# A two-layer Mamba-2 / gated-MLP encoder step on one core: one residual step, one row of mixer units and two sets of norm sums change places

## Chip, cores and metric

The kernel runs on one core of one Trainium2 chip. The metric is the device time of one execution in microseconds (us), the median over several runs.

## What is computed

One inference step over 576 frames: 512 of a new stream and 64 of a running one. Two layers, each a token mixer and a squared-ReLU feed-forward network (FFN), each followed by a residual and a LayerNorm. Cut to what matters here (float32 throughout, `x` is 576 x 1024):

```
# layer 0: Mamba-2 state-space mixer, 8 groups of 4 heads
proj = x @ w_in; z, xbc, dt = split(proj)
xbc  = silu(causal_conv4(xbc) + b)
y, h = ssd_scan(xs, softplus(dt + dt_bias), A, B, C, h0)     # chunked scan
g    = (y + d * xs) * silu(z)
g    = g * rsqrt(mean(g*g over the group) + eps) * norm_w
x    = layer_norm(alpha * x + g @ w_out)                      # norm 0
x    = layer_norm(alpha * x + square(relu(x @ w1)) @ w2)      # norm 1
# layer 1: chunked spatial-gating mixer
u, v = split(gelu(x @ w_in + b_in)); v = layer_norm(v)
s    = tril(w_s) @ v (per 128-row block and group) + b_s
x    = layer_norm(alpha * x + (u * s) @ w_out)                # norm 2
x    = layer_norm(alpha * x + square(relu(x @ w1)) @ w2)      # norm 3
```

## The kernel before

**Layout.** Features lie on the 128 partitions, the 576 frames (`T`) along the free axis, split into two halves of 288 (`HT`). A weight unit is 128 x 1024: eight 128 x 128 blocks. Each float32 operand is split into a high and a low part, and TensorE (PE) makes a product of three matmuls: high by high, weight-high by data-low, weight-low by data-high (`products`, L627 to L629). A unit is therefore 2 halves x 8 blocks x 3 = 48 matmuls of 288 columns.

**PSUM slots.** Unit `u` writes the slot `u % 2`: two banks, 0 and 1 or 2 and 3. Before it starts, PE waits until its weights are split (`w_ready`) and until the unit two before it has been read out of the slot (`slot_evac0` or `slot_evac1`). Banks 4 to 7 serve the state-space chunks, the spatial products and the sums of the norms. Weights come from HBM through SP's queue into a ring of four buffers; POOL splits them from the last state-space group on.

**Order.** Every engine has its own program, written out by hand, and works through it strictly in that order; semaphores tie them together. Three places matter.

*The last state-space group* (`group(GROUPS - 1, False)` in the programs of VectorE, DVE, and of PE). While the last chunks run, PE already computes the first units of `w_out` (`U_WOUT + 0` to `+ 5`, `nxt(j)` in PE's `group`). DVE reads each of them out with `residual_first` (L1617 adds the slot to alpha times the input's high part and frees the slot, L1620 adds the low part). After the last chunk (`after(g, 4)`, up to L1579) DVE runs `gate` (L1591, y * silu(z)), then the residual step of unit 3, then `sum_squares` (L1596), which waits for ScalarE's (ACT's) square of the gated rows. PE's unit 5 needs the slot of unit 3. PE's `mean_squares(g)` follows its unit 5 and needs `sum_squares`.

*The mixer of layer 1* (end of PE's program, `mix`, `norm_v`, `uv_low` on DVE, `u_gelu`, `uv_round` on ACT). `gate_unit(k)` gives the u columns of tile k, `spatial(k)` (L936 to L938, small float32 matmuls into banks 4 to 7) the mixed v columns. PE runs gate unit 2, the row sums of the spatial weights (L946), then for k = 0 to 15: the gate unit k+1 from k = 2 on, the first unit of the output product, `U_CMOUT`, at k = 15, and `spatial(k)`. For each k DVE runs `mix(k)` (L2027, L2030, L2032, L2038), then `norm_v(k + 2)` (L2012), which makes the operand of a later `spatial`, and, once ACT has rounded the product (L1350), `uv_low(k)` (L2044). Only behind the whole loop stands DVE's `block(U_CMOUT, "first")`, which reads out the units of the output product with the same `residual_first` (L1617, L1620):

```
    for k in range(16):
        mix(k)
        ...
        uv_low(k)
    block(U_CMOUT, "first")
```

*The first unit after a norm* (`first_unit(n, u)` for norms n = 0, 1, 2). The LayerNorm is applied after the product, so PE starts on unnormalised columns. The first unit runs half 0, then `deferred_sums(n)`, four float32 matmuls with a block of ones (L655 and L657, each once per half) that add up sums and sums of squares over the partitions, then half 1 (two columns wider). ACT and DVE make the mean and the reciprocal deviation from them (L1191 to L1196, L1777 to L1782); DVE's `normalized` (L1894) needs both before it frees the slot of the unit.

Of the kernel before, what the change touches and what calls it, by code (L numbers as in the profile page):

```python
# [13 lines left out]
KT = D // P  # L14
# [29 lines left out]
U_CMOUT = U_U + 16 - EARLY  # L44
# [28 lines left out]
def slot_turn(u):  # L73

    return (u if u < U_V else u - 16) // 2
# [3 lines left out]
def ssd_unit(g, j):  # L79

    return U_SSD + 6 * (g + 1) + j
# [3 lines left out]
def gate_unit(k):  # L85

    return U_E + k if k < EARLY else U_U + k - EARLY
# [313 lines left out]
def wait(engine, sem, value):  # L401

    if not isinstance(value, int) or value > 0:
        engine.wait_ge(sem, value)
# [35 lines left out]
def ext_half(t, k, h):  # L440

    return t[:, k, 0:HT] if h == 0 else t[:, k, HT:TX]
# [177 lines left out]
def tensor_program(pe, m, A):  # L620
# [3 lines left out]
    def products(out, w, k, x, start, stop):  # L624

        w_hi, w_lo = m.wh[:, w, k * P:(k + 1) * P], m.wl[:, w, k * P:(k + 1) * P]
        mm(out, w_hi, x[0], start=start, stop=False)  # L627
        mm(out, w_hi, x[1], start=False, stop=False)  # L628
        return mm(out, w_lo, x[0], start=False, stop=stop)  # L629

    def unit(u, w, turn, xh, xl, half=half_of):

        s = w % 2
        pe.wait_ge(S.w_ready, u + 1)
        wait(pe, m.slot_evac[s], turn)
        for h, k in [(h, k) for h in range(2) for k in range(KT)]:
            x = half(xh, k, h), half(xl, k, h)
            last = products(m.ps[:, 2 * s + h, 0:x[0].shape[-1]], w, k, x, k == 0, k == KT - 1)
        last.then_inc(S.gemm_done, 1)

    def run_few(u0, n, xh, xl, half=half_of):
        for u in range(u0, u0 + n):
            unit(u, u % RING, slot_turn(u), xh, xl, half=half)
# [7 lines left out]
    def deferred_sums(n):  # L651

        for h in range(2):
            pe.wait_ge(S.sum1_ready, 10 * n + 8 + 2 * h)
            mm(m.ps[:, 4 + h, 0:HT], m.ones[:, :], m.s1[:, h], start=True, stop=True)  # L655
            pe.wait_ge(S.sum2_ready, 10 * n + 8 + 2 * h)
            last = mm(m.ps[:, 6 + h, 0:HT], m.ones[:, :], m.s2[:, h], start=True, stop=True)  # L657
        last.then_inc(S.d_sums, 1)
# [54 lines left out]
    def first_unit(n, u):  # L713

        s = u % 2
        for h in range(2):
            pe.wait_ge(S.xt_lo, 10 * n + 8 + 2 * h)
            if h == 0:
                pe.wait_ge(S.w_ready, u + 1)
                pe.wait_ge(m.slot_evac[s], slot_turn(u))  # L720
            else:
                deferred_sums(n)
                pe.wait_ge(S.ext_lo, n + 1)
            for k in range(KT):
                x = ext_half(m.xh_ext, k, h), ext_half(m.xl_ext, k, h)
                last = products(m.ps[:, 2 * s + h, 0:x[0].shape[-1]], u % RING, k, x, k == 0, k == KT - 1)
        last.then_inc(S.gemm_done, 1)
# [204 lines left out]
    def spatial(k, j, ws):  # L932

        pe.wait_ge(S.vm_ready, k + 1)
        for t in range(4):
            mm(m.ps[:, 4 + 2 * j, t * BLK:(t + 1) * BLK], m.vm[:, j, t, :], ws, start=True, stop=True)  # L936
        mm(m.ps[:, 5 + 2 * j, 0:TS], m.vm[0:TS, j, 4, :], ws[0:TS, 0:TS], start=True, stop=True)  # L937
        mm(m.ps[:, 5 + 2 * j, TS:2 * TS], m.vm[0:TS, j, 4, :], m.ident[0:TS, 0:TS],  # L938
           start=True, stop=True).then_inc(S.mix_done, 1)
# [5 lines left out]
    for b in range(2):  # L945
        last = mm(m.ps[:, 6 + b, :].rearrange("p (g t) -> p g t", t=BLK), m.ones[:, :], m.wst[:, 4 * b:4 * b + 4, :],  # L946
                  start=True, stop=True)
    last.then_inc(S.wsum_done, 1)
    for k in range(16):
        if 1 < k < 15:  # L950
            run_few(gate_unit(k + 1), 1, m.hh, m.hl)
        elif k == 15:
            pe.wait_ge(S.uv_lo, 8)
            run_few(U_CMOUT, 1, m.xh, m.xl)
        if k == 1:
            pe.wait_ge(S.wsum_ready, 1)
        spatial(k, k % 2, m.wst[:, k // 2, :])
    run_few(U_CMOUT + 1, 7, m.xh, m.xl)
    pe.wait_ge(S.uv_lo, 16)
    last_block(2, U_CMOUT + 8, m.hh[:, 8:16], m.hl[:, 8:16])  # L960
    ffn(1, U_FFN1)
# [406 lines left out]
def vector_program(dve, m, A):  # L1368
# [3 lines left out]
    def weight_lo(u):  # L1372

        s = u % RING
        dve.wait_ge(S.w_ready, u)
        dve.wait_ge(S.w_hi, u + 1)
        tt(m.wl[:, s], m.wraw[:, s], m.wh[:, s], ALU.subtract).then_inc(S.w_ready, 1)  # L1377
# [64 lines left out]
    def conv(g, j):  # L1442

        s = (U_SSD + j) % 2
        u = U_SSD + j
        r, a = m.raw[:, j % 2], m.acc[:, j]
        turn = slot_turn(u)
        dve.wait_ge(m.slot_evac[s], 3 * g + (turn + 1))
        dve.wait_ge(S.cpar_ready, g + 1)
        for b, at in enumerate((TP, RAW - HALO)):  # L1450
            dst = m.ctail[:, g, j, b] if isinstance(g, int) else \
                m.ctail[:, bass.ds(g, 1), j, b].rearrange("p a c -> p (a c)")
            cp(dst, r[:, at:at + HALO]).then_inc(S.ctail_ready, 1)
        if j == 0:
            wait(dve, S.silu_ready, 4 * g)
            dve.wait_ge(S.raw_zero, 1)
        ts(a, r[:, 0:CONV], m.cpar[:, j, 0:1], m.cpar[:, j, 4:5], ALU.mult, ALU.add).then_inc(S.conv_tap, 1)
        for k in range(1, 4):
            dve.wait_ge(S.conv_tap, 16 * g + (4 * j + k))
            stt(a, r[:, k:k + CONV], m.cpar[:, j, k:k + 1], a, ALU.mult, ALU.add).then_inc(S.conv_tap, 1)  # L1460
# [15 lines left out]
    def window(g):  # L1476

        dve.wait_ge(S.win_exp, g + 1)
        tt(m.dtw[:, :, :], m.gdt[:, :, :], m.win[:, :, :], ALU.mult).then_inc(S.dtw_ready, 1)
# [31 lines left out]
    def before(g, n):  # L1511

        t0, q = cols(n)
        k = n % 2
        if n == 0:
            dve.wait_ge(S.acb_in, 16 * g + 16)
            dve.wait_ge(S.gdt_ready, 2 * g + 2)
            wait(dve, S.s_done, 5 * g)
        if n >= 2:
            dve.wait_ge(S.s_done, 5 * g + (n - 1))  # L1520
        for e in range(HPG):
            last = ts(m.dec[0:q, k, e, 0:q], m.acb[0:q, e, t0:t0 + q], m.gac[0:q, ORDER[n], e:e + 1], 0.0,
                      ALU.subtract, ALU.min)
        last.then_inc(S.dec_arg, 1)
# [59 lines left out]
    def gate(g):  # L1584

        for j in range(2):
            s = (U_SSD + 4 + j) % 2
            dve.wait_ge(m.slot_evac[s], 3 * g + (slot_turn(U_SSD + 4 + j) + 1))
        dve.wait_ge(S.y_evac, 4 * g + 4)
        wait(dve, S.yn_lo, g)  # L1590
        tt(m.gy[:, :, :], m.y[:, :, :], m.zs[:, :, :], ALU.mult).then_inc(S.gate_ready, 1)  # L1591
# [19 lines left out]
    def residual_first(u0, i, j, k=None, x=(m.xh, m.xl)):  # L1611

        u = u0 + j
        s = u % 2
        k = 2 * i + j if k is None else k
        dve.wait_ge(S.gemm_done, 2 * i + (u + 1))
        stt(halves(one(m.r, k)), halves(one(x[0], k).bitcast(F32)), ALPHA, bank_pair(m, s),  # L1617
            ALU.mult, ALU.add).then_inc(m.slot_evac[s], 1)
        dve.wait_ge(m.slot_evac[s], i + (slot_turn(u) + 1))
        stt(one(m.r, k), one(x[1], k).bitcast(F32), ALPHA, one(m.r, k), ALU.mult, ALU.add  # L1620
            ).then_inc(S.res_ready, 1)

    def group(g, more, first=False):
        def nxt(j):

            if more:
                conv(g + 1, j)
            else:
                residual_first(U_WOUT, 0, j, j)

        before(g, 0)
        before(g, 1)
        if not first:
            weight_lo(ssd_unit(g, 0))
        weight_lo(ssd_unit(g, 1))
        if not first:
            window(g)
            skip_params(g)
            norm_params(g - 1)
        operands(g, 0)  # L1640
        operands(g, 1)
        weight_lo(ssd_unit(g, 2))
        weight_lo(ssd_unit(g, 3))
        if more:
            conv_params(g + 1)
        after(g, 0)
        before(g, 2)
        after(g, 1)
        operands(g, 2)
        if not first:  # L1650
            scale(g - 1)
        nxt(0)
        before(g, 3)
        after(g, 2)
        operands(g, 3)
        weight_lo(ssd_unit(g, 4))
        nxt(1)
        before(g, 4)
        after(g, 3)
        operands(g, 4)  # L1660
        weight_lo(ssd_unit(g, 5))
        if not first:
            split(g - 1)
        nxt(2)
        after(g, 4)
        gate(g)
        nxt(3)
        sum_squares(g)
        if more:
            group_columns(g + 1)  # L1670
        else:
            norm_params(g)
            nxt(4)
            nxt(5)
            scale(g)
            split(g)
# [322 lines left out]
    for t in range(NTOK):  # L1999
        n = TS if t == 4 else P  # L2000
# [201 lines left out]
```

## Time and profile before

| what | value |
|---|---|
| median of 3 runs | 1701.09 us (1700.87 to 1701.17) |
| the profiled execution's own time | 1701.2 us |
| its span in the profile | 1699.5 us, 31397 instructions |
| PE busy | 1679.0 us (99% of the span) |
| DVE, ACT, POOL busy | 919.5 us (54%), 518.0 us (30%), 696.6 us (41%) |
| DMA | 148.11 MB, 87 GB/s on average |
| granted PE clock, mean | 0.997 of full speed |

How to read it: the span is the time between the first and last instruction of the profiled execution; 1.7 us of its own time lie around it. PE's busy share counts matmuls from start to modelled end, and neighbours overlap, so waits inside the stream are read from the starts in the timeline and from the view of the waits.

### The profile page before, as it was taken

The page shows a single profiled execution, that of the slowest core. Times are in us where ns is not written, and L with a number is a line of the kernel's source. Part 1 is how long each engine was busy: PE and PEld are TensorE (multiplying, and loading weights), DVE is VectorE, ACT ScalarE, POOL GpSimd, SP SyncE. Part 2 cuts the span into 40 slices and gives each one's busy share as a digit, 9 for nine tenths or more (in the row PEclk, how much of TensorE's full clock was granted, in tenths as well). Part 3 has the DMA queues.
Part 4 walks back from the last instruction along what each step waited for, and adds up shares of the span by engine and source line. Part 5 has one row for each costly group of instructions (what it writes and reads, how often), then busy time and mean ns, then how long its engine had stood idle before and what let it go on. Part 6 is the DMA issues. An engine that isn't in the chain of part 4 may idle for free.

```text
span 1699.5 us, 31397 instructions
## 1 busy us (share of the span) xinstructions
PE 1679.0 (99%) x12274; PEld 1625.5 (96%) x12274; DVE 919.5 (54%) x1719; ACT 518.0 (30%) x871; POOL 696.6 (41%) x577
## 2 busy tenths in 40 slices
PE   9999999999999999999999999999999999999996
PEld 9999999999999999999999888999999999999996
DVE  7788999888756441312226715886265431313225
ACT  4455545555124430302202502111024321303105
POOL 0000000000456565565555365454555565555552
PEclk9999999999999999999999999999999999999998
DMA  5223332323222222222222322222222222222222
GB/s 197 82 90 100 104 108 95 101 69 97 72 87 76 87 79 83 87 76 86 86 75 87 124 76 85 68 66 71 83 87 75 85 76 87 80 81 87 78 84 68
DMA packets 46438, 148.11 MB, mean 87 GB/s; under 512 B 7297, under 2 KB 13057, under 8 KB 45185
## 3 DMA queue, kind: packets, MB, share of 16 engines
q1 hardware_dynamic: 37888, 129.98, 23.1%
q10 hardware_dynamic: 8448, 16.69, 3.1%
q8 instruction: 74, 1.21, 0.3%
q14 instruction: 28, 0.22, 0.0%
HBM read 141.50 MB, written 5.15 MB: 86 GB/s over the span
## 4 chain that ended last, share of the span: by engine, by line
PE 71%; DVE 2%; ACT 1%; issue 0%; ACTq 0%; DVEq 0%
PE ps L627 21%; PE ps L628 21%; PE ps L629 21%; PE ps L882 2%; PE ps L883 2%; PE ps L884 2%; PE ps L936 1%; DVE s L1707 0%; PE ps L937 0%; PE ps L892 0%; PE ps L893 0%; PE ps L938 0%; DVE gy L1591 0%; ACT r L1254 0%; DVE vm L2012 0%
## 5 line engine op out<-in xcount | busy, mean ns | idle before, releaser
L627 PE MATMUL ps<-xh,wh 128*128 128x288 f32 (+1 forms) x1968 | 585.9, 298 | 0.8 <-DVE xl L1381 0.7
L628 PE MATMUL ps<-xl,wh 128*128 128x288 f32 (+1 forms) x1968 | 583.3, 296 | 0.0
L629 PE MATMUL ps<-xh,wl 128*128 128x288 f32 (+1 forms) x1968 | 583.1, 296 | 0.0
L627 PE MATMUL ps<-h,wh 128*128 128x288 f32 x1632 | 482.7, 296 | 1.4 <-DVE r L1617 1.4
L629 PE MATMUL ps<-h,wl 128*128 128x288 f32 x1632 | 480.8, 295 | 0.0
L628 PE MATMUL ps<-h,wh 128*128 128x288 f32 x1632 | 480.6, 294 | 0.0
L549 POOL TENSOR_TENSOR wl<-wraw,wh 128x1024 fp32r<-128x1024 f32 x184 | 448.6, 2438 | 15.3
L546 POOL TENSOR_TENSOR tick<-tick 128x1 f32<-128x1 f32 x184 | 44.2, 240 | 922.3 <-DMA wraw<-wstream 489.8
L627 PEld LDWEIGHTS ps<-xh,wh 128*128 128x128 f32 x1968 | 372.2, 189 | 1.8 <-issue 1.5
L629 PEld LDWEIGHTS ps<-xh,wl 128*128 128x128 f32 x1968 | 371.3, 189 | 0.0
L628 PEld LDWEIGHTS ps<-xl,wh 128*128 128x128 f32 x1968 | 370.8, 188 | 0.2
L627 PEld LDWEIGHTS ps<-h,wh 128*128 128x128 f32 x1632 | 306.1, 188 | 2.6 <-issue 1.6
L628 PEld LDWEIGHTS ps<-h,wh 128*128 128x128 f32 x1632 | 306.1, 188 | 0.1
L629 PEld LDWEIGHTS ps<-h,wl 128*128 128x128 f32 x1632 | 306.1, 188 | 0.0
L1690 DVE TENSOR_TENSOR r<-ps,r 128x576 f32 (+1 forms) x70 | 53.1, 758 | 317.3 <-PE ps L629 304.0
L547 POOL TENSOR_SCALAR wh<-wraw 128x1024 fp32r<-128x1024 f32 x184 | 198.5, 1079 | 0.0
L1894 DVE SCALAR_TENSOR_TENSOR ta<-mean,cd,ps 128x576 f32<-128x576 f32 x64 | 52.1, 814 | 236.2 <-ACT cd L1284 236.2
L1284 ACT ACTIVATE cd<-ps 128x2 f32<-128x2 f32 x64 | 11.0, 171 | 331.0 <-PE ps L629 331.0
L1286 ACT ACTIVATE rl<-ta,cd 128x576 f32<-128x576 f32 x64 | 49.9, 779 | 115.9 <-DVE ta L1897 115.9
L1460 DVE SCALAR_TENSOR_TENSOR acc<-raw,cpar,acc 128x579 f32<-128x579 f32 x96 | 79.0, 823 | 3.4
L1377 DVE TENSOR_TENSOR wl<-wraw,wh 128x1024 fp32r<-128x1024 f32 x55 | 67.0, 1218 | 1.5 <-ACT wh L979 1.0
L979 ACT ACTIVATE wh<-wraw 128x1024 fp32r<-128x1024 f32 x55 | 58.4, 1062 | 17.9 <-DMA wraw<-wstream 17.5
(241 smaller groups left out, 1723.7 us busy)
## 6 DMA issues: line engine op xcount, KB each, us to landing
wraw<-wstream SPq DMA_DIRECT2D x240, 512.0 KB, 3.4
acb<-acum_scratch ACTq DMA_DIRECT2D x8, 1152.0 KB, 6.0
out_y<-r SPq DMA_DIRECT2D x8, 288.0 KB, 2.3
xr<-x ACTq DMA_DIRECT2D x4, 288.0 KB, 6.4
xr<-x SPq DMA_DIRECT2D x4, 288.0 KB, 6.2
hs<-ssm_in ACTq DMA_DIRECT2D x8, 128.0 KB, 6.0
out_ssm_s<-hsn ACTq DMA_DIRECT2D x8, 128.0 KB, 5.6
out_ssm_p<-hp ACTq DMA_DIRECT2D x8, 128.0 KB, 1.9
```

Source lines behind the costliest of these rows:

```text
L546: pool.tensor_tensor(m.tick[:, 1:2], m.tick[:, 0:1], m.tick[:, 0:1], ALU.add)
L547: pool.tensor_scalar(m.wh[:, s], m.wraw[:, s], 1.0, 1.0, ALU.mult, ALU.mult).then_inc(S.w_hi, 1)
L549: pool.tensor_tensor(m.wl[:, s], m.wraw[:, s], m.wh[:, s], ALU.subtract).then_inc(S.w_ready, 1)
L627: mm(out, w_hi, x[0], start=start, stop=False)
L628: mm(out, w_hi, x[1], start=False, stop=False)
L629: return mm(out, w_lo, x[0], start=False, stop=stop)
L979: f(m.wh[:, u % RING], m.wraw[:, u % RING], ACT.Copy).then_inc(S.w_hi, 1)
L1286: f(m.rl[:, j], m.ta[:, j], ACT.Relu, bias=m.cd[:, j, 1:2], scale=-1.0).then_inc(S.rl_ready, 1)
L1377: tt(m.wl[:, s], m.wraw[:, s], m.wh[:, s], ALU.subtract).then_inc(S.w_ready, 1)
L1460: stt(a, r[:, k:k + CONV], m.cpar[:, j, k:k + 1], a, ALU.mult, ALU.add).then_inc(S.conv_tap, 1)
L1690: tt(r, bank_pair(m, s), r, ALU.add).then_inc(m.slot_evac[s], 1)
L1894: stt(halves(ta), m.mean[:, :, :], m.cd[:, j, 0:1], bank_pair(m, u % 2), ALU.mult, ALU.subtract).then_inc(m.slot_evac[u % 2], 1)
```

## The change

It touches the programs of PE and DVE; the instructions stay the same in number and shape, only their places change.

1. In the last state-space group DVE runs the residual step of `U_WOUT + 3` ahead of `gate` in place of behind it.
2. In the mixer PE runs `gate_unit(3)` right behind the row sums, ahead of `spatial(0)`, and every later gate unit one place further forward. The first unit of the output product comes before `spatial(14)` in place of `spatial(15)`, its second before `spatial(15)`, and six follow the loop in place of seven.
3. For norms 0 and 2 the four sums go from between the halves of the first unit to the middle of its second half, behind 12 of its 24 matmuls. Norm 1 is left as it was.

```diff
@@ first_unit(n, u)
             else:
-                deferred_sums(n)
+                if n == 1:
+                    deferred_sums(n)
                 pe.wait_ge(S.ext_lo, n + 1)
             for k in range(KT):
+                if n != 1 and (h, k) == (1, KT // 2):
+                    deferred_sums(n)
@@ tensor_program, mixer
     last.then_inc(S.wsum_done, 1)
+    run_few(gate_unit(3), 1, m.hh, m.hl)
     for k in range(16):
-        if 1 < k < 15:
-            run_few(gate_unit(k + 1), 1, m.hh, m.hl)
-        elif k == 15:
+        if 1 < k < 14:
+            run_few(gate_unit(k + 2), 1, m.hh, m.hl)
+        elif k == 14:
             pe.wait_ge(S.uv_lo, 8)
             run_few(U_CMOUT, 1, m.xh, m.xl)
+        elif k == 15:
+            run_few(U_CMOUT + 1, 1, m.xh, m.xl)
         if k == 1:
             pe.wait_ge(S.wsum_ready, 1)
         spatial(k, k % 2, m.wst[:, k // 2, :])
-    run_few(U_CMOUT + 1, 7, m.xh, m.xl)
+    run_few(U_CMOUT + 2, 6, m.xh, m.xl)
@@ vector_program, group(g, more)
-        gate(g)
-        nxt(3)
+        if more:
+            gate(g)
+            nxt(3)
+        else:
+            nxt(3)
+            gate(g)
```

**PE at the end of the mixer** (behind L629 the last spatial product, k = 15; `xh` is here the rounded u * s, `vm` the normalised v). Before, the unit behind it is the second of the output product:

```order
L628 MATMUL ps<-xl,wh 128x288
L629 MATMUL ps<-xh,wl 128x288
L936 MATMUL ps<-wst,vm 128x128 [waits vm_ready]
L936 MATMUL ps<-wst,vm 128x128 x3
L937 MATMUL ps<-wst,vm 128x64
L938 MATMUL ps<-ident,vm 128x64
L627 MATMUL ps<-xh,wh 128x288 [waits slot_evac0,w_ready]
L628 MATMUL ps<-xl,wh 128x288
L629 MATMUL ps<-xh,wl 128x288
```

With the change (L939 to L941 are the lines of `spatial`) it is the third:

```order
L628 MATMUL ps<-xl,wh 128x288
L629 MATMUL ps<-xh,wl 128x288
L939 MATMUL ps<-wst,vm 128x128 [waits vm_ready]
L939 MATMUL ps<-wst,vm 128x128 x3
L940 MATMUL ps<-wst,vm 128x64
L941 MATMUL ps<-ident,vm 128x64
L627 MATMUL ps<-xh,wh 128x288 [waits slot_evac1,w_ready]
L628 MATMUL ps<-xl,wh 128x288
L629 MATMUL ps<-xh,wl 128x288
```

The unit behind the last spatial product now waits for slot 1, which holds the first unit of the output product, where it waited for slot 0, which held the last gate unit.

**DVE at the end of the last state-space group** (`gy` is the gated y, `r` the residual). Before:

```order
L1578 TENSOR_TENSOR y<-y,yo 128x2x128 [waits yo_ready,y_skip,hdec_ready]
L1579 TENSOR_TENSOR hp<-ps,hdec 128x256
L1591 TENSOR_TENSOR gy<-y,zs 128x1152 [waits y_evac,yn_lo,slot_evac0,slot_evac1]
L1617 SCALAR_TENSOR_TENSOR r<-xh,ps 128x576 [waits gemm_done]
L1620 SCALAR_TENSOR_TENSOR r<-xl,r 128x576 [waits slot_evac0]
L1596 TENSOR_TENSOR y<-y 128x576 [waits sq_ready]
L1491 COPY normw<-pv 128x2 [waits yn_f]
```

With the change (lines are six further down):

```order
L1584 TENSOR_TENSOR y<-y,yo 128x2x128 [waits yo_ready,y_skip,hdec_ready]
L1585 TENSOR_TENSOR hp<-ps,hdec 128x256
L1623 SCALAR_TENSOR_TENSOR r<-xh,ps 128x576 [waits gemm_done]
L1626 SCALAR_TENSOR_TENSOR r<-xl,r 128x576 [waits slot_evac0]
L1597 TENSOR_TENSOR gy<-y,zs 128x1152 [waits y_evac,yn_lo,slot_evac0,slot_evac1]
L1602 TENSOR_TENSOR y<-y 128x576 [waits sq_ready]
L1497 COPY normw<-pv 128x2 [waits yn_f]
```

The two rows of the residual step, the first of which frees a slot of PE's, now stand ahead of the gate.

**PE at the sums of norm 0** (the 290-column rows are the second half of the first FFN unit). Before:

```order
L627 MATMUL ps<-xh,wh 128x288
L628 MATMUL ps<-xl,wh 128x288
L629 MATMUL ps<-xh,wl 128x288
L655 MATMUL ps<-s_98,ones 128x288 [waits sum1_ready,xt_lo]
L657 MATMUL ps<-s_99,ones 128x288 [waits sum2_ready]
L655 MATMUL ps<-s_98,ones 128x288 [waits sum1_ready]
L657 MATMUL ps<-s_99,ones 128x288 [waits sum2_ready]
L627 MATMUL ps<-xh,wh 128x290 [waits ext_lo]
L628 MATMUL ps<-xl,wh 128x290
```

With the change:

```order
L627 MATMUL ps<-xh,wh 128x290
L628 MATMUL ps<-xl,wh 128x290
L629 MATMUL ps<-xh,wl 128x290
L655 MATMUL ps<-s_98,ones 128x288 [waits sum1_ready]
L657 MATMUL ps<-s_99,ones 128x288 [waits sum2_ready]
L655 MATMUL ps<-s_98,ones 128x288 [waits sum1_ready]
L657 MATMUL ps<-s_99,ones 128x288 [waits sum2_ready]
L627 MATMUL ps<-xh,wh 128x290
L628 MATMUL ps<-xl,wh 128x290
```

The sums now stand between the fourth and the fifth block of the second half, and the half itself waits only for `xt_lo` and `ext_lo`. Norm 2 moves in the same way.

## Rows read from the trace of the kernel before

**Rows 1.** Waits of PE, whole span: total us, times, longest us.
```profile
PE ps L627 <- DVE r L1617: 1.4, 1, 1.4
PE ps L655 <- DVE s L1707: 1.1, 3, 0.4
PE ps L936 <- DVE vm L2012: 0.9, 1, 0.9
```

**Rows 2.** Timeline of PE, last state-space group: start, length, line, tiles, shape.
```profile
444.17 0.29 PE L629 MATMUL ps<-h,wl 128*128 128x288 f32 x1
445.86 0.37 PE L627 MATMUL ps<-h,wh 128*128 128x288 f32 x1 [1.40 <-DVE r L1617]
446.06 0.30 PE L628 MATMUL ps<-h,wh 128*128 128x288 f32 x1
```

**Rows 3.** Timeline of DVE, last state-space group.
```profile
441.83 3.22 DVE L1591 TENSOR_TENSOR gy<-y,zs 128x1152 f32<-128x1152 f32 x1
444.97 0.74 DVE L1617 SCALAR_TENSOR_TENSOR r<-xh,ps 128x576 f32<-128x576 f32 x1
445.75 0.76 DVE L1620 SCALAR_TENSOR_TENSOR r<-xl,r 128x576 f32<-128x576 f32 x1
446.42 0.75 DVE L1596 TENSOR_TENSOR y<-y 128x576 f32<-128x576 f32 x1
```

**Rows 4.** Timeline of PE, first unit after norm 0.
```profile
520.08 0.65 PE L655 MATMUL ps<-s,ones 128*128 128x288 f32 x2
520.56 0.65 PE L657 MATMUL ps<-s,ones 128*128 128x288 f32 x2
521.49 0.75 PE L655 MATMUL ps<-s,ones 128*128 128x288 f32 x2 [0.28 <-DVE s L1707]
522.08 0.65 PE L657 MATMUL ps<-s,ones 128*128 128x288 f32 x2
...
525.78 0.30 PE L627 MATMUL ps<-xh,wh 128*128 128x288 f32 x1
```

**Rows 5.** Timeline of PE, sums of norm 2, the first and last of four.
```profile
1273.47 0.65 PE L655 MATMUL ps<-s,ones 128*128 128x288 f32 x2
...
1275.62 0.65 PE L657 MATMUL ps<-s,ones 128*128 128x288 f32 x2
```

**Rows 6.** Timeline of DVE, norm 0.
```profile
518.82 2.62 DVE L1707 TENSOR_TENSOR s<-s,r 128x288 f32<-128x288 f32 x1
521.36 0.44 DVE L1713 TENSOR_TENSOR s<-s,sqm 128x288 f32<-128x288 f32 x1
...
524.24 1.25 DVE L1779 TENSOR_SCALAR msq<-msq 128x576 f32<-128x576 f32 x1
...
529.09 0.81 DVE L1894 SCALAR_TENSOR_TENSOR ta<-mean,cd,ps 128x576 f32<-128x576 f32 x1
```

**Rows 7.** Timeline of PE, start of the mixer.
```profile
1056.03 1.88 PE L946 MATMUL ps<-wst,ones 128*128 128x512 f32 x4
1058.76 1.16 PE L936 MATMUL ps<-wst,vm 128*128 128x128 f32 x8 [0.85 <-DVE vm L2012]
```

**Rows 8.** Timeline of PE, the first matmul behind the last spatial product.
```profile
1174.59 0.40 PE L627 MATMUL ps<-xh,wh 128*128 128x288 f32 x1
```

**Rows 9.** Timeline of DVE, the same place.
```profile
1174.70 0.75 DVE L2027 SCALAR_TENSOR_TENSOR sb<-ps,pv,sbias 128x512 f32<-128x512 f32 x1 [3.98 <-PE ps L938]
...
1177.31 1.33 DVE L2044 TENSOR_TENSOR h<-sb,h 128x576 fp32r<-128x576 f32 x1 [0.75 <-ACT h L1350]
1178.56 0.74 DVE L1617 SCALAR_TENSOR_TENSOR r<-h,ps 128x576 f32 x1
```

**Rows 10.** Durations of L2044's later tiles: min, median, max ns.
```profile
L2044 DVE TENSOR_TENSOR h<-sb,h x8: 759/759/1327, 1126.3 to 1177.3; 128x576 fp32r<-128x576 f32 x8
```

**Rows 11.** Windows at the end: us, busy per engine, granted PE clock, DMA.
```profile
1686.00:1688.00 2.00, 0.00 (x0) 0.00 (x0) 1.24 (x4) 1.43 (x5) 0.80 (x1) 1.00 0.51 186
...
1689.00:1690.00 1.00, 0.00 (x0) 0.00 (x0) 0.00 (x0) 0.99 (x3) 0.00 (x0) 0.62 0.00 0
```

## The prediction

> **What bounds the kernel now.** PE is busy almost without a break, so I read three views in turn: the list of PE's waits, to see where its stream breaks at all; the timeline around each place the change touches, to price the break; and the timelines of the engine that ends the break, to see what will end it afterwards. The list has three entries that belong to this change, 1.4, 1.1 and 0.9 us [rows 1]; they sit exactly at its three places. So the change can win a few microseconds out of 1700 and no more: the matmuls are the same, in number and shape. What decides is whether the new order opens a wait that the old one covered.
>
> **Part 1, the last state-space group.** PE's last matmul of a unit starts at 444.17, the next would start 0.13 later, at 444.30; it starts at 445.86, and its successor comes 0.20 behind it in place of 0.13 [rows 2]. That is 1.63 us lost. What ends it is the first step of the residual, which frees the slot: DVE starts it at 444.97, behind a gate of 3.22 us [rows 3]. Run ahead of the gate it would start where the gate starts now, 441.83, and end 0.74 later, at 442.57. From its end now (445.71) to PE's start is 0.15, so PE could go on at 442.72, 1.58 before it needs to. The whole 1.63 goes, and the spare time is too wide for this term to be much smaller.
> The price is a later gate. It moves behind two steps of 0.74 and 0.76, so to about 443.4. At its present length it ends at 446.6 in place of 445.05; the square and the sum behind it end 2.12 later (447.17 now) [rows 3], at 448.7. PE needs that sum after the 48 matmuls of the unit it started at 444.30, at 0.133 each 6.4 us, so at 450.7. Two microseconds are left: hidden. Everything behind the sum hangs on PE's own matmul of it, and moves with PE.
>
> **Part 2, the start of the mixer.** The row sums of the spatial weights start at 1056.03 [rows 7]. A float32 matmul of 288 columns takes PE 0.48 (start to start, [rows 4]); two of 512 columns take in proportion 0.48 x 512 / 288 x 2 = 1.71, so PE is free at 1057.74, and the spatial product starts at 1058.76, when DVE has the normalised tile [rows 7]. Lost: 1.02. With the gate unit in between, of 6.4 us, the tile is there long before. A return from float32 matmuls to the products happens once more; its first matmul shows 0.40 against 0.30 [rows 2, 8], which takes 0.1 back. Net gain 0.92; the list's own 0.9 [rows 1] less 0.1 is the lower bound, 1.02 the upper. No DMA is moved; SP's loads wait for PE's units and POOL's splits for the loads, unit by unit, so the weights keep their lead. The later tiles keep their distances: between two spatial products there is one unit, as before, and a gate unit's read-out by ACT now comes earlier with respect to its use.
>
> **Part 2, the end of the mixer.** Here the cover goes. DVE reads out the first unit of the output product only behind the whole loop, that is behind `mix(15)` and `uv_low(15)`, which need the last spatial product. Now a whole unit, the second, stands on PE between that product and the unit that needs the slot of the first. With the change the second unit stands ahead of the last spatial product, and the unit right behind it, the third, waits for that slot. PE's next matmul starts at 1174.59 [rows 8]; DVE starts on the product at 1174.70, and after `mix`, ACT's rounding and the low part starts the residual step at 1178.56, which ends 0.74 later, at 1179.30 [rows 9]. With the 0.15 of part 1 PE would go on at 1179.45. The chain is the same after the change: its engines were idle when it began (DVE had waited 3.98, [rows 9]). So PE waits 1179.45 - 1174.59 = 4.86 us. One link may be shorter: the low part took 1.33 here, its median is 0.76 [rows 9, 10]; without that, 4.29 is the lower bound. I take 4.86, since what made it slow, POOL's split of the next weights, follows the end of a unit that stands the same way ahead of the product in both orders.
>
> **Part 3, the sums of norms 0 and 2.** The four sums start at 520.08 and, 0.48 apart, would end at 522.00. The third starts at 521.49 and the fourth at 522.08, so they end at 522.56 [rows 4]: 0.56 lost, because DVE's last sum took 2.62 and ended at 521.44 [rows 6]. For norm 2 they start at 1273.47, would end at 1275.39 and end at 1276.10 [rows 5]: 0.71. Together 1.27. Twelve products, 1.6 us, put the sums at 521.68; DVE's two are done by 521.80, before the third and fourth are up. Nothing is left of the wait.
> The price: the sums end at 521.68 + 1.92 = 523.60, 1.04 later, and so does what is made of them. DVE's read-out of the first unit ends at 529.90 now [rows 6], then 530.94. PE needs the slot after the second unit: that starts at 525.78 now [rows 4], 0.56 earlier then, and lasts 6.4, so at 531.62. Left: 0.7, for norm 2 about as much (0.9 later, 0.7 earlier). I cost it at nothing; if DVE loses more time beside POOL on the way (the 1.25 of L1779, [rows 6], shows that it does), PE waits up to half a microsecond at each of the two places.
>
> **The sum.** -1.63 - 0.92 + 4.86 - 1.27 = +1.04 us on the profiled execution's own 1701.2, so 1702.2. That execution is 0.1 above the median of 1701.09, so I forecast a median of 1702.1, 0.06% up. A measurement of this kernel can tell about 0.2% from no change, 3.4 us, so 1697.7 to 1704.5 is no change. With the terms' bounds (stall 4.29, two extra waits of 0.5) this case alone runs from 1701.4 to 1703.1; slips of a transfer or a split by up to a microsecond make it 1700.5 to 1704.
>
> **Rivals.**
> *The clock falls in the new wait.* At its end the kernel shows what PE's clock does when PE is idle: no matmul runs from 1686 on, the granted clock is 1.00 (2.4 GHz) up to 1688 and on average 0.62 in the window from 1689 to 1690, so it falls to its lower level, 1.2 GHz, there [rows 11]. The new wait of 4.86 is longer than PE had then been idle. Against it: that is one fall in one place, and waits up to 1.4 us left no trace on the clock [rows 1]. If it falls, the matmuls behind the wait run at double spacing for a while. No row has a matmul at the lower level; the bounds are nothing (it falls too late or recovers at once) and a whole unit at double spacing, 6.4. I take the middle, 24 matmuls, 3.2: 1705.3, slower. It decides once more than 2.4 us are lost, 18 matmuls at double spacing.
> The Trainium skill (TensorE: Matmul & The Clock Gate, "HAM oscillation — how this bites in real kernels") speaks against this change by that mechanism: it tells of kernels whose waits between bursts of matmuls let the clock drop to half, so that each burst starts cold. By that rule the result is this rival's; the tail agrees with it, and no run so far shows it in mid-kernel.
> *The wait at the end of the mixer does not come,* because the read-out is earlier than the old trace lets one see. Then only the gains are left: 1701.1 - 3.8 = 1697.3, faster. For it speaks only that DVE has spare time there; against it that its program holds the read-out behind the last `mix`, whatever else is free.
> *The later sums push the FFN's read-out over the edge,* with an extra wait of about 1 us at both norms: 1704.1, still no change.
>
> **How the numbers follow.** Forecast 0.60; clock 0.26; no new wait 0.06; later sums 0.08. The clock's price is open from 0 to 6.4, so a little over half of its chance, 0.15, lies above 1704.5; 0.01 of the third rival joins it. Slower 0.16, faster 0.06, same 0.78. The range leaves out the no-wait case below and the dear half of the clock case above: 1699.5 to 1705.5.
>
> **What would show it.** In the profile after: PE's list of waits loses the 1.4 and the 0.9 and two of the three waits for L1707's sums, and gains one entry of 4 to 5 us behind DVE's residual step, right behind the last spatial product. The granted clock just behind that entry decides between the forecast and the first rival. If that entry is under 2 us, my reading of DVE's order is wrong; if PE also waits in the third unit of an FFN, the cover of part 3 was too thin.

## The result, and the profile after

Median 1703.93 us over 20 runs (1703.25 to 1704.86), against 1701.05 over 20 runs of the kernel before (1700.56 to 1701.51): ratio 1.0017, 95% interval [1.0011, 1.0023], or 2.9 us more. That is inside the range, and the median is inside what was called no change (0.2%), on its slow side; the interval reaches 0.23%. The profiled execution took 1703.46 with a span of 1701.7, 2.2 above before.

PE's list of waits after the change (total us, times, longest) answers to [rows 1]:

```profile
PE ps L627 <- DVE r L1623: 4.8, 1, 4.8
PE ps L756 <- POOL eps L582: 1.5, 1, 1.5
PE ps L627 <- DVE xl L1387: 1.5, 2, 0.9
PE ps L885 <- DVE h L1820: 1.1, 1, 1.1
PE ps L655 <- DVE s L1717: 0.4, 1, 0.4
```

The old 1.4 and 0.9 are gone, of three waits for sums the one of norm 1 is left, and one entry is new: 4.8, behind the residual step (L1623 is the old L1617). The entry for `xl` lies in the first microseconds, while the input loads; it was 0.7 before, and other runs below show 0.4 to 1.7 for it.

*Last state-space group*, DVE and then PE, against [rows 2, 3]:

```profile
441.73 0.74 DVE L1623 SCALAR_TENSOR_TENSOR r<-xh,ps 128x576 f32<-128x576 f32 x1
442.50 1.85 DVE L1626 SCALAR_TENSOR_TENSOR r<-xl,r 128x576 f32<-128x576 f32 x1
444.27 1.34 DVE L1597 TENSOR_TENSOR gy<-y,zs 128x1152 f32<-128x1152 f32 x1
446.85 0.76 DVE L1602 TENSOR_TENSOR y<-y 128x576 f32<-128x576 f32 x1 [1.23 <-ACT y L1147]
```

```profile
444.29 0.29 PE L627 MATMUL ps<-h,wh 128*128 128x288 f32 x1
```

The slot is free at 442.47 and PE goes on at 444.29, where it would without any wait. The gate starts 2.4 us later than before but ends only 0.6 later (445.61 against 445.05), because it took 1.34 where it took 3.22. POOL's split of a weight unit ran at the same place in both kernels, first before, then after:

```profile
441.39 2.44 POOL L549 TENSOR_TENSOR wl<-wraw,wh 128x1024 fp32r<-128x1024 f32 x1
```

```profile
441.28 2.45 POOL L549 TENSOR_TENSOR wl<-wraw,wh 128x1024 fp32r<-128x1024 f32 x1
```

Before, the gate ran beside it; now the residual's second step does and takes 1.85 in place of 0.76, while the gate starts after the split's end. (The residual's first step keeps its 0.74 beside the split.) The sum behind the gate ends at 447.61, 0.4 later than before, 3 us ahead of PE's need.

*Norm 0*, PE and then DVE, against [rows 4, 6]:

```profile
520.04 0.65 PE L655 MATMUL ps<-s,ones 128*128 128x288 f32 x2
520.53 0.65 PE L657 MATMUL ps<-s,ones 128*128 128x288 f32 x2
521.01 0.65 PE L655 MATMUL ps<-s,ones 128*128 128x288 f32 x2
521.50 0.65 PE L657 MATMUL ps<-s,ones 128*128 128x288 f32 x2
...
530.03 0.30 PE L627 MATMUL ps<-xh,wh 128*128 128x288 f32 x1
```

```profile
523.66 0.46 DVE L1789 TENSOR_SCALAR msq<-msq 128x576 f32<-128x576 f32 x1
...
527.71 0.81 DVE L1904 SCALAR_TENSOR_TENSOR ta<-mean,cd,ps 128x576 f32<-128x576 f32 x1
```

The four sums follow one another at 0.48 without a break. The step that took 1.25 before takes 0.46, and the read-out of the first FFN unit ends at 528.52, 1.5 us before PE's third unit at 530.03. POOL's split before and after shows what the step escaped:

```profile
522.79 2.39 POOL L549 TENSOR_TENSOR wl<-wraw,wh 128x1024 fp32r<-128x1024 f32 x1
```

```profile
521.25 2.38 POOL L549 TENSOR_TENSOR wl<-wraw,wh 128x1024 fp32r<-128x1024 f32 x1
```

Before, the split ended at 525.18, in the middle of the step (524.24 to 525.49). Now it ends at 523.63, 0.03 us before the step starts.

*The mixer's start*, PE, against [rows 7]: the gate unit stands directly behind the row sums, and the spatial product waits for nothing.

```profile
1053.78 1.88 PE L949 MATMUL ps<-wst,ones 128*128 128x512 f32 x4
1055.10 0.70 PE L627 MATMUL ps<-h,wh 128*128 128x288 f32 x1
...
1061.87 1.05 PE L939 MATMUL ps<-wst,vm 128*128 128x128 f32 x8
```

*The mixer's end*, PE and then DVE, against [rows 8, 9]:

```profile
1177.29 0.38 PE L941 MATMUL ps<-ident,vm 64*128 64x64 f32 x2
1182.53 0.58 PE L627 MATMUL ps<-xh,wh 128*128 128x288 f32 x1 [4.85 <-DVE r L1623]
...
1183.38 0.44 PE L627 MATMUL ps<-xh,wh 128*128 128x288 f32 x1
1184.10 0.44 PE L627 MATMUL ps<-xh,wh 128*128 128x288 f32 x1
...
1186.46 0.29 PE L627 MATMUL ps<-xh,wh 128*128 128x288 f32 x1
1186.86 0.29 PE L627 MATMUL ps<-xh,wh 128*128 128x288 f32 x1
```

```profile
1177.72 0.75 DVE L2037 SCALAR_TENSOR_TENSOR sb<-ps,pv,sbias 128x512 f32<-128x512 f32 x1 [4.09 <-PE ps L941]
...
1180.32 1.40 DVE L2054 TENSOR_TENSOR h<-sb,h 128x576 fp32r<-128x576 f32 x1 [0.75 <-ACT h L1356]
1181.64 0.74 DVE L1623 SCALAR_TENSOR_TENSOR r<-h,ps 128x576 f32 x1
```

The chain on DVE is the one foreseen, link by link, and PE stands still from about 1177.6 to 1182.53. What follows was not in the forecast's sum: rows of the same line, three matmuls apart, come every 0.72 us at first and every 0.40 from 1186 on. The windows of the same stretch say why. A row gives the window and its length in us, the busy time (with the number of instructions) of PE, of PE's weight load, of DVE, ACT and POOL, then the granted clock, DMA's share and GB/s:

```profile
1181.00:1182.00 1.00, 0.00 (x0) 0.00 (x0) 1.00 (x2) 0.00 (x0) 0.92 (x2) 1.00 0.00 0
1182.00:1183.00 1.00, 0.47 (x2) 0.50 (x3) 0.85 (x2) 0.00 (x0) 1.00 (x1) 0.69 0.00 0
1183.00:1184.00 1.00, 1.00 (x6) 1.00 (x5) 1.00 (x1) 0.00 (x0) 0.94 (x1) 0.50 0.00 0
1184.00:1185.00 1.00, 1.00 (x6) 1.00 (x5) 1.00 (x2) 0.00 (x0) 0.00 (x0) 0.50 0.00 0
1185.00:1186.00 1.00, 1.00 (x7) 1.00 (x6) 0.85 (x2) 0.00 (x0) 0.00 (x0) 0.60 0.00 0
1186.00:1188.00 2.00, 2.00 (x17) 2.00 (x16) 0.12 (x1) 0.00 (x0) 0.00 (x0) 1.00 0.00 0
```

The granted clock fell to half (1.2 GHz) late in the wait and came back only after some three microseconds of matmuls. What that left is read from two later places. Before, the third output unit and the first product of norm 2 start at

```profile
1181.07 0.30 PE L627 MATMUL ps<-xh,wh 128*128 128x288 f32 x1
...
1270.27 0.29 PE L627 MATMUL ps<-xh,wh 128*128 128x288 f32 x1
```

and after the change the first starts at 1182.53, the second at

```profile
1273.25 0.29 PE L627 MATMUL ps<-xh,wh 128*128 128x288 f32 x1
```

### The profile page after: what moved, and what is told of

It reads as the page before. It is cut to its first block, busy times and chain, and to the rows that moved or that the text cites. A ratio compares the mean times of both kernels' runs of the same rounds, so it can differ in the third digit from the quotient of the medians.

```text
span 1701.7 us, 31397 instructions
## 1 busy us (share of the span) xinstructions
PE 1678.7 (99%) x12274; PEld 1626.5 (96%) x12274; DVE 920.1 (54%) x1719; ACT 518.9 (30%) x871; POOL 693.5 (41%) x577
## 4 chain that ended last, share of the span: by engine, by line
PE 97%; DVE 1%; ACT 1%; DMA 0%; issue 0%; ACTq 0%; DVEq 0%
PE ps L627 28%; PE ps L628 28%; PE ps L629 28%; PE ps L885 2%; PE ps L886 2%; PE ps L887 2%; PE ps L804 1%; PE ps L808 1%; PE ps L801 1%; PE ps L939 1%; PE ps L783 1%; PE ps L781 1%; PE ps L816 0%; PE ps L940 0%; DMA xr<-x 0%; PE ps L895 0%
## 5 line engine op out<-in xcount | busy, mean ns | idle before, releaser
L629 PE MATMUL ps<-xh,wl 128*128 128x288 f32 (+1 forms) x1968 | 583.7, 297 | 0.0
L629 PE MATMUL ps<-h,wl 128*128 128x288 f32 x1632 | 480.9, 295 | 0.0
L629 PEld LDWEIGHTS ps<-xh,wl 128*128 128x128 f32 x1968 | 371.8, 189 | 0.0
L629 PEld LDWEIGHTS ps<-h,wl 128*128 128x128 f32 x1632 | 306.1, 188 | 0.0
```

## The experiments

**Theory.** The gains are as priced; the loss is the uncovered read-out at the mixer's end, 4.9 us, and the lower clock behind it. **Rivals.** The parts take something from one another or cost elsewhere what they gain; units one place forward hurt by themselves; the slow matmuls are slow for another reason than the clock. Ratios below are to the kernel before, with their 95% interval; its median in these sets was 1701.0 to 1701.2. Differences in us are those of the medians. The ratios lie up to 0.06% away from those of the medians, mostly below, as the kernel before, run 74 times there, took 1704.8 to 1705.4 in five of them.

**Parts 1 and 3 without the mixer's part.** Edit: the kernel before, with the new DVE order and the later sums.

> Only the residual step ahead of the gate and the later norm sums; the mixer as before. My theory (these two parts gain 1.6 and 1.25 us, all the loss is in the mixer): 1698.2 us, 2.9 below the kernel before, no wait of PE for the gate's residual step and one wait for sums left. Rival (the later sums or the later gate cost elsewhere what they gain): 1700.5 or more.

Measured: 1698.28 us (1697.94 to 1698.44), ratio 0.9979 [0.9970, 0.9988]: faster by 2.9. PE's list has neither the residual step nor the sums of norms 0 and 2 in it; the spatial product's entry is still there:

```profile
PE ps L939 <- DVE vm L2019: 1.0, 1, 1.0
...
PE ps L655 <- DVE s L1714: 0.4, 1, 0.4
```

The two parts give back nothing: 2.9 is what the two terms of the prediction add up to.

**The mixer's part alone.** Edit: the kernel before, with only the hunk of the mixer.

> Only the mixer's part of the change. My theory (gain 1.1 at its start, a wait of 4.9 at its end, 1.5 to 2.4 for the lower clock behind it): 1706.4 to 1707.3 us, 5.3 to 6.2 above the kernel before. Rival (the parts hinder one another, the mixer alone costs only its wait): 1705 or less.

Measured: 1706.83 us (1706.25 to 1707.41), ratio 1.0030 [1.0019, 1.0040]: 5.7 more. With the run above, -2.9 + 5.7 = +2.8, the whole change within 0.1: the parts do not hinder one another.

**The residual step alone, and the sums alone.** Edits: one hunk each.

> Only the residual step ahead of the gate. My theory: 1.6 us gained, 1699.5 us; the wait of 1.4 gone, the product of the group's mean squares not delayed. Rival (the later gate delays the mean squares): 1700.5 or more.

Measured: median 1699.47 us, ratio 0.9991 [0.9982, 1.0001], 1.6 less than the 1701.08 of its set.

> Only the later sums of norms 0 and 2. My theory: 1.25 us gained, 1699.9 us; of three waits for DVE's sums one is left. Rival (the read-out of the first FFN units comes too late and takes part of it back): 1700.4 or more, with a wait of PE in the third unit.

Measured: median 1699.79 us, ratio 0.9993 [0.9984, 1.0002], 1.3 less. Each interval alone just takes in no change, so neither gain is shown by its times alone. But the two medians add up to the 2.9 of both together, which is clear of no change, and each profile has lost its own waits.

**Output unit put back on PE.**

```diff
-        elif k == 14:
+        elif k == 15:
             pe.wait_ge(S.uv_lo, 8)
             run_few(U_CMOUT, 1, m.xh, m.xl)
-        elif k == 15:
-            run_few(U_CMOUT + 1, 1, m.xh, m.xl)
...
-    run_few(U_CMOUT + 2, 6, m.xh, m.xl)
+    run_few(U_CMOUT + 1, 7, m.xh, m.xl)
```

> The whole change, but the first unit of the output product back between the last two spatial products and the second behind the loop; so the products 13 and 14 stand side by side. My theory (the loss is the uncovered read-out at the mixer's end, nothing else): no wait there, clock 1.00 throughout, 1697.1 us, 4 below the kernel before. Rival (units one place forward hurt by themselves, by weights or by the normalised tiles): 1699 or more, with a wait ahead of product 14 or 15.

Measured: 1697.17 us (1697.04 to 1697.26), ratio 0.9971 [0.9960, 0.9983]: 4.0 less than the kernel before and faster than both. PE works through the mixer's end without a gap at full clock; two of the windows there, of 5 us each (those up to 1190 also have PE at 5.00 and the clock at 1.00):

```profile
1165.00:1170.00 5.00, 5.00 (x40) 5.00 (x39) 5.00 (x8) 0.00 (x0) 2.57 (x2) 1.00 0.02 3
1170.00:1175.00 5.00, 5.00 (x39) 4.81 (x38) 3.50 (x7) 1.37 (x2) 1.46 (x3) 1.00 0.44 118
```

So the early gate units do no harm, and all of the loss is in the last two places of the loop. Against the first run it also isolates the mixer's start: 1698.28 - 1697.17 = 1.1.

**The read-out moved on DVE instead.** The same loss, attacked from the other side: PE's order as changed, DVE's read-out ahead of `mix(15)`.

```diff
     for k in range(16):
+        if k == 15:
+            residual_first(U_CMOUT, 0, 0, x=(m.hh, m.hl))
         mix(k)
...
-    block(U_CMOUT, "first")
+    residual_first(U_CMOUT, 0, 1, x=(m.hh, m.hl))
+    with dve.Fori(1, 4) as i:
+        residual_first(U_CMOUT, i, 0, x=(m.hh, m.hl))
+        residual_first(U_CMOUT, i, 1, x=(m.hh, m.hl))
```

> The changed kernel with DVE's read-out of the first output unit ahead of mix(15), in DVE's idle time, instead of behind uv_low(15); PE's order as changed. My theory (DVE's order makes the wait): no wait behind the last spatial product, clock 1.00, 1697.1 us, as with the output unit put back. Rival (PE's order itself is the loss): above 1699.

Measured: 1697.23 us (1696.99 to 1697.48), ratio 0.9978 [0.9968, 0.9987]. There is no wait at the place; the third output unit starts right behind the last spatial product:

```profile
1177.54 0.40 PE L627 MATMUL ps<-xh,wh 128*128 128x288 f32 x1
```

With PE's changed order left alone the loss is gone: PE's new order loses nothing by itself, it is the place of the read-out in DVE's order that makes it wait.

**The wait filled.** The changed kernel, with matmuls put into the wait whose result is not used.

```diff
+    pe.wait_ge(S.uv_ready, 15)
+    for n in range(5):
+        mm(m.ps[:, 4, :].rearrange("p (g t) -> p g t", t=BLK), m.ones[:, :], m.wst[:, 0:4, :], start=True, stop=True)
     run_few(U_CMOUT + 2, 6, m.xh, m.xl)
```

> The changed kernel with five float32 matmuls of 512 columns, about 4.3 us, put into PE's wait behind the last spatial product; their result is not used. My theory (the lower clock behind the wait costs 1.5 to 2.4 us): the wait stays, the clock stays at 1.00, the units behind it run at 0.133 us a matmul at once, 1701.5 to 1702.4 us, below the changed kernel although PE has more to do. Rival (the slow matmuls behind the wait come from weights or memory, not from the clock): 1703.9 or more.

Measured: 1702.04 us (1701.89 to 1702.33), ratio 1.0002 [0.9993, 1.0011]; none of its runs reaches the fastest of the changed kernel (1703.25). PE's timeline, then the windows:

```profile
1177.71 4.56 PE L966 MATMUL ps<-wst,ones 128*128 128x512 f32 x10
1182.61 0.37 PE L627 MATMUL ps<-xh,wh 128*128 128x288 f32 x1 [0.35 <-DVE r L1626]
1183.09 0.29 PE L627 MATMUL ps<-xh,wh 128*128 128x288 f32 x1
```

```profile
1182.00:1183.00 1.00, 0.65 (x4) 0.42 (x4) 0.85 (x2) 0.00 (x0) 1.00 (x1) 1.00 0.00 0
1183.00:1184.00 1.00, 1.00 (x9) 1.00 (x9) 1.00 (x1) 0.00 (x0) 1.00 (x1) 1.00 0.00 0
```

The third output unit starts as late as in the changed kernel (1182.61 against 1182.53), with the same weights, and POOL's split beside it is as long (2.75 against 2.74); but the clock is 1.00, and with it the spacing 0.13. More work, 1.9 us less. The slow matmuls were the clock's.

**The wait shortened.** Two versions that put the read-out between `mix(15)` and `uv_low(15)`, and inside `mix(15)` ahead of its last step; otherwise as in the run on DVE's order.

> The changed kernel with that read-out between mix(15) and uv_low(15): the wait is shortened, not removed, to 0.12 + 1.86 + 0.74 + 0.15 = 2.9 us. If a wait of this length leaves the clock at 1.00: 1697.1 + 2.9 = 1700.0 us. Rival (any wait of some microseconds lowers the clock, with 1.5 us or more behind it): 1701.5 or more.

Measured: 1701.38 us, ratio 0.9999 [0.9989, 1.0008]. Two of 11 runs lie at 1699.9, the others from 1701.0 to 1701.5. My own number, 1700.0, is that of the two; the rest lie at, or up to half a microsecond below, the rival's 1701.5. The mean granted clock goes with it: 0.997 in the two, 0.996 in the nine. The profile is of one in which the clock fell:

```profile
1180.35 0.37 PE L627 MATMUL ps<-xh,wh 128*128 128x288 f32 x1 [2.71 <-DVE r L1623]
```

```profile
1180.00:1181.00 1.00, 0.65 (x5) 0.68 (x6) 0.97 (x2) 0.26 (x1) 1.00 (x1) 1.00 0.15 33
1181.00:1182.00 1.00, 1.00 (x6) 1.00 (x6) 1.00 (x2) 0.00 (x0) 0.92 (x2) 0.52 0.00 0
1182.00:1183.00 1.00, 1.00 (x6) 1.00 (x5) 1.00 (x1) 0.00 (x0) 1.00 (x1) 0.50 0.00 0
```

Here PE had been at work again for over half a microsecond when the clock fell.

> The changed kernel with the read-out of the first output unit inside mix(15), behind its three steps that read the product and ahead of the last: the wait shrinks to 0.12 + 1.1 + 0.74 + 0.15 = 2.1 us. If the clock can fall in any wait of 2 us or more: 1697.2 + 2.1 + 1.4 = 1700.7 us in most runs. If this one is too short for it: 1699.3 us in all of them, and the clock stays at 1.00.

Measured: 1700.83 us, ratio 0.9995 [0.9986, 1.0004]; three of 11 runs from 1699.15 to 1699.4 (mean granted clock 0.997), eight from 1700.75 to 1701.0 (0.996). Both expected numbers are there, side by side, the two groups some 1.6 us apart. The profiled run is one of those without the fall:

```profile
1179.75 0.37 PE L627 MATMUL ps<-xh,wh 128*128 128x288 f32 x1 [2.04 <-DVE r L1623]
```

```profile
1180.00:1181.00 1.00, 1.00 (x9) 1.00 (x9) 1.00 (x2) 0.00 (x0) 1.00 (x2) 1.00 0.00 0
```

So, judged by time and mean clock, even a wait of about 2.0 us costs the clock in most runs, though not in all; none of the eight is profiled. What decides in which is not settled: the kernel is the same.

## Why the prediction was right, and where it was not

The verdict held: no change by more than 0.2%, a little slower. It did not hold by the forecast's own case, a clock that stays, which would have given 1702.1. It held because the fall of the clock, which came, cost 1.9 us, and not the 3.2 that the prediction gave it; from 2.4 on the prediction itself would have called the result slower. As no row had a matmul at the lower clock, that part is luck. By its steps:

| term | forecast, us | measured, us | from |
|---|---|---|---|
| part 1, residual step ahead | -1.63 | -1.6 | residual step alone |
| part 3, later sums | -1.27 | -1.3 | sums alone |
| part 2, mixer's start | -0.92 | -1.1 | parts 1 and 3 against output unit put back |
| part 2, new wait at the mixer's end | +4.86 | +4.9 | wait filled less output unit put back, 1702.04 - 1697.17 |
| lower clock behind that wait | 0 (rival: +3.2) | +1.9 | changed kernel less wait filled, 1703.93 - 1702.04 |
| sum | +1.0 | +2.8 | (the whole change: +2.9) |

- *The gains* are the old waits, as read from the starts. The covers named for the later gate and the later sums held, with more to spare than I gave them: the gate and the step of norm 0 that took 1.25 had run beside POOL's split and moved out from beside it. That was not foreseen, and at norm 0 the margin was 0.03 us.
- *The new wait* came as priced: the chain of the old trace, from 1174.70 to 1179.30 [rows 9], came again link by link.
- *The step that failed* is the forecast's case itself. "Against it: that is one fall in one place" was my reason to hold a fall of the clock in the wait for the less likely case, at 0.26. It came in the profile, and no run of the changed kernel lies near 1702.1: the fastest is 1703.25. The rival was right in mechanism and mis-sized in its price: I took 24 matmuls at double spacing, 3.2 us; the runs show 1.9 in the median. In the profiled run the third output unit starts 1.5 later than in the kernel before (1182.53 against 1181.07) and the first product of norm 2 three microseconds later (1273.25 against 1270.27), so 1.5 was lost in between, close to what some 13 matmuls at double spacing cost. The price seems to vary from run to run: the changed kernel's runs spread over 1.6 us, against 0.95 in the 20 of the kernel before, and those with a mean granted clock of 0.996 took 1703.25 to 1703.6, those with 0.995 took 1703.5 to 1704.9.
- *The third rival*, extra waits in the FFN, did not come: L1779's 1.25, read as a sign that DVE loses time there, was time beside one POOL split, and in the new order that split was just over (0.46).

The Trainium skill (TensorE: Matmul & The Clock Gate, "HAM oscillation — how this bites in real kernels") names the mechanism, waits of PE after which the next matmuls start at half clock. The changed kernel agrees: behind its wait of 4.85 us the granted clock is 0.50 in the first full microsecond of matmuls. Behind the wait of 2.7 us it differs: there the matmuls start at full clock and slow down only when PE has been at work for over half a microsecond.

## What to carry to other kernels

Moving work forward on one engine uncovers whatever it stood in front of: for every PSUM slot ask not only what PE runs meanwhile, but also where the read-out stands in the program of the engine that does it, and behind what. Here the row of units could go forward at its start and stay put at its end, which gained 1.1 us where the whole row moved lost 5.7. On a PE that is otherwise almost never idle, price a new wait with its clock as well: here, behind waits of 2.0 to 4.9 us, it cost another 1.5 to 2 us where the clock fell, and matmuls that nobody needs, put into the longest, brought that back.

## What was not expected of the hardware

The clock fell behind shorter waits than the one at the kernel's end suggested. There PE had been idle from 1686 on [rows 11], and in the kernel before the clock was still full up to 1689:

```profile
1688.00:1689.00 1.00, 0.00 (x0) 0.00 (x0) 0.00 (x0) 0.98 (x2) 0.00 (x0) 1.00 0.26 92
```

In the middle of the stream a wait of 2.7 us was enough in 9 of 11 runs, by their times and mean clocks, and one of 2.0 us in 8 of 11. In the one fall of these that is profiled, it came when PE was already at work again.

Behind the waits of 1.1 and 1.4 us in the profile of the kernel before the granted clock is 1.00. But five of its 74 runs in the sets of the experiments took 1704.8 to 1705.4, some 4 us more than the median, at a mean granted clock of 0.995; the runs near the median have 0.997. None of the five is profiled, so where the clock fell in them, and whether one of these waits had to do with it, stays open.
